# One block with 64 experts: half of the columns of each down projection as a split product of three fp32r matmuls, the other half left in fp32

## The chip, the cores and the metric

The kernel runs on one core of one Trainium2 chip. The metric is the device time of one execution in microseconds, the median of three runs. In the profile PE is the matrix engine (TensorE), PEld its weight loads, DVE VectorE, ACT ScalarE, POOL GpSimd, and SP the queue that issues the large loads from HBM.

## The reference

One layer over 512 tokens of 1024 values. First a mixing sub-layer (gated MLP beside stick-breaking attention), then the part that takes most of the time: a mixture of 64 experts, 8 of them for each token.

```python
h = rmsnorm(x, g_pre_ffn) * (1.0 + sc2) + sh2
gates = route(h, w_router, router_bias)            # 8 of 64 experts for each token
g = einsum('sd,edf->sef', h, w_gate)               # w_gate, w_up: (64, 1024, 256)
u = einsum('sd,edf->sef', h, w_up)
act = silu(g) * u * gates[:, :, None]
y = einsum('sef,efd->sd', act, w_down)             # w_down: (64, 256, 1024)
y = y + (silu(h @ ws_gate) * (h @ ws_up)) @ ws_down
x = x + ga2 * rmsnorm(y, g_post_ffn)
```

Everything is float32, and the three weights of an expert are 1 MB each.

## The kernel before

The five engines have their programs written out by hand, with semaphores between them. The experts are worked through as **blocks** of up to 128 rows: one block for each of the 64 experts, and further ones where an expert has more than 128 tokens. In this run there are 68 blocks. A block is `(i, s)` with number `b = 2i + s`, and `s` (0 or 1, `SLOTS = 2`) says which of two buffers it uses. `after(i, s, d)` is the block `d` further on, `num` its number.

What happens to block b:

1. SP (`refill`) loads the gate and up weights into `raw[:, s]` as soon as both halves of the low parts of block b-2 have been made (`split_done`: semaphores `lo_dve` and `lo_pool`). Right behind, in the same call, it loads the **down weights of block b-2** into `rawd[:, s]`, once the down projection of b-4 is over (`dn_mm`).
2. POOL gathers the rows of h for the block (`gather`, L580), by indices that DVE makes from a one-hot product (`tables`, `onehot`).
3. PE transposes the rows (`rows_in`, helper line L947). ACT takes their high part `hthi` (L859, a cast to fp32r), DVE the low part `htlo` (L1675).
4. ACT casts the raw gate and up weights to fp32r in two halves (`high`, L827: `whi`); DVE makes three quarters of each low half (`low`, L1661: `raw - whi`) and POOL the last quarter (`low_rest`, L595).
5. PE runs the **split product** (`gate_up`, L1213 to L1215): for each of 8 k tiles `hthi x whi`, `hthi x wlo`, `htlo x whi`, each a 128x512 fp32r matmul.
6. ACT applies silu (L855), DVE multiplies (L1668: `act_s`), PE transposes (`acts_tr`), ACT copies the result out of PSUM (`act_rows`, L863: `actt`).
7. PE runs the down projection (`down`, L1232): four fp32 matmuls of 128x512, two k tiles for each half of the 1024 columns, straight from `rawd`. The profile records each of them as two.
8. ACT copies the rows out (`y_out`, L869), POOL scatters them to `y_rows` (`scatter`, L588).

The engines are at different blocks in one step. The order of a step on each is fixed by these calls:

```python
# PE, block_pe(b)
rows_in(b+1); indices(b+3); gate_up(b, 0, 3); acts_tr(b-1); gate_up(b, 3, 8); down(b-1)
# ACT, step_act(b)
y_out(b-3); ht_high(b); high(b, 0); act_rows(b-2); high(b, 1); silu(b-1)
# DVE, step_dve(b)
rows_of(b-3); ht_low(b); tables(b+2); onehot(b+3); low(b, 0); low(b, 1); times_up(b-1)
# POOL, step_pool(b)
scatter(b-3); gather(b+2); low_rest(b, 0); low_rest(b, 1)
# SP, refill(b)
split_done(b-2); load gate, up (b); wait dn_mm >= b-3; load down (b-2)
```

So ACT, DVE and POOL work at step b while PE is in `block_pe(b-1)`. Each engine takes its list strictly in order.

Of the kernel before, what the change touches and what calls it, by code (L numbers as in the profile page):

```python
# [61 lines left out]
def block_kernel(nc, x, c, w_ada, b_ada, g_pre_mix, w_in, ln_sgu_g, ln_sgu_b, w_spatial, b_spatial,  # L62
                 g_branch, w_out, g_post_mix, g_pre_ffn, w_router, router_bias, w_gate, w_up,
                 w_down, ws_gate, ws_up, ws_down, g_post_ffn, out):
    with ExitStack() as ctx:
        def sem(name):
            return ctx.enter_context(nc.semaphore(name))
# [4 lines left out]
        def at(name, shape, dt, off):  # L72
            return nc.alloc_sbuf_tensor_at(name, shape, dt, offset=base + off)
# [3 lines left out]
        raw = at("raw", [P, SLOTS, 2, 2048], F32, 0)  # L77
        rawd = at("rawd", [P, SLOTS, KF, D], F32, 32 * KB)
        whi = at("whi", [P, SLOTS, 2, 2048], F32R, 48 * KB)
        wlo = [at("wlo0", [P, 2, 2048], F32R, 96 * KB), at("wlo1", [P, 2, 2048], F32R, 80 * KB)]  # L80
# [84 lines left out]
        act_s = small("act_s", [P, KF, P], F32)  # L165
        actt = at("actt", [P, KF, P], F32, 184 * KB)
        sht = at("sht", [P, 2, KF, P], F32, 64 * KB)

# [156 lines left out]
        at_tr = sem("at_tr")  # L325
        actt_ok = sem("actt_ok")
        dn_mm = sem("dn_mm")
        y_ok = sem("y_ok")
# [327 lines left out]
        def _(ac):  # L656
# [204 lines left out]
            def act_rows(i, s):  # L861
                ac.wait_ge(at_tr, num(i, s) + 1)
                A(actt[:, :, :], bank(3)[:, 0:F].rearrange("p (k q) -> p k q", k=KF), ACT.Copy).then_inc(actt_ok, 1)  # L863

            def y_out(i, s):
# [5 lines left out]
            def step_act(i, s, late):  # L871

                if late >= 3:
                    y_out(*after(i, s, -3))
                ht_high(i, s)
                high(i, s, 0)
                if late >= 2:
                    act_rows(*after(i, s, -2))
                high(i, s, 1)
                silu(*after(i, s, -1))  # L880
# [47 lines left out]
            last = m + (E // 2 - 1)  # L928
            y_out(m + (E // 2 - 2), 1)
            act_rows(last, 0)  # L930
            silu(last, 1)
            y_out(last, 0)
            act_rows(last, 1)
            y_out(last, 1)

# [7 lines left out]
        def _(pe):  # L943
# [281 lines left out]
            def down(i, s):  # L1225
                pe.wait_ge(wd_in[s], i * 16 + 16)
                pe.wait_ge(actt_ok, num(i, s) + 1)
                if not (isinstance(i, int) and num(i, s) == 0):
                    pe.wait_ge(y_ok, num(i, s))
                for hf in range(2):  # L1230
                    for k in range(KF):
                        ins = mm(bank(4 + hf), actt[:, k, :], rawd[:, s, k, hf * 512:(hf + 1) * 512],  # L1232
                                 start=(k == 0), stop=(k == KF - 1))
                ins.then_inc(dn_mm, 1)
# [68 lines left out]
        def _(v):  # L1303
# [354 lines left out]
            def low(i, s, half):  # L1658
# [3 lines left out]
                                ALU.subtract).then_inc(lo_dve, 1)  # L1662

            def times_up(i, s):

# [16 lines left out]

            def step_dve(i, s, late=True):
                if late:
                    rows_of(*after(i, s, -3))
                ht_low(i, s)
                tables(*after(i, s, 2))
                onehot(*after(i, s, 3))
                low(i, s, 0)
                low(i, s, 1)  # L1690
                times_up(*after(i, s, -1))
# [14 lines left out]
            over_tables()  # L1706
            step_dve(0, 1, late=False)
            step_dve(1, 0, late=False)
            for b in range(3, 6):
# [6 lines left out]
            with v.If(m > 0):  # L1716
                with v.Fori(E // 2, m + E // 2) as i:
                    for s in range(SLOTS):
                        step_dve(i, s)
            rows_of(m + (E // 2 - 2), 1)  # L1720
            times_up(m + (E // 2 - 1), 1)
            rows_of(m + (E // 2 - 1), 0)
            rows_of(m + (E // 2 - 1), 1)
# [43 lines left out]
```

## Time and profile before

| what | value |
|---|---|
| median of the runs | 1160.01 us (1159.15 to 1163.89) |
| the profiled execution | 1166.54 us, its span 1164.8 us |
| PE busy | 1007.2 us, 86% of the span |
| DVE / ACT / POOL busy | 744.7 / 569.7 / 615.8 us |
| DMA queue q1 (the loads of SP) | 267.41 MB |
| share of the chain that ended last | PE 75%, DVE 12%, DMA 4% |
| costliest line of that chain | L1232, the down projection, 19% |
| PE clock granted, mean of the span | 0.939 of 2.4 GHz |

The span runs from the first instruction to the last. A busy share tells only how much an engine had to do over the whole of it. The chain that ended last is followed back from the last instruction, and tells what the end waited for. From about 396 us to about 1076 us the kernel is in the loop over blocks.

### The profile page before, as it was taken

To read this page: it belongs to the slowest core of one execution; us is meant where nothing else is said; L and a number is where in the kernel's file an instruction comes from. 1 tells how busy PE (TensorE), PEld (TensorE's weight loads), DVE (VectorE), ACT (ScalarE), POOL (GpSimd) and SP (SyncE) were. 2 spreads that over 40 slices of the span, in tenths; PEclk is the share of its full clock that TensorE was granted. 3 is DMA by queue.
4 is the path that set the end of the run, shared out by engine and by line. 5 is a ranking of instruction groups with operands and counts; after the bars stand their busy time and mean duration, and the time that the engine had idled before them with its cause. 6 is when DMAs were issued, how large, how long until landed. Compare 5 with 4: busy or idle time off the path is not lost.

```text
span 1164.8 us, 14917 instructions
## 1 busy us (share of the span) xinstructions
PE 1007.2 (86%) x4420; PEld 711.0 (61%) x4420; DVE 744.7 (64%) x1287; ACT 569.7 (49%) x604; POOL 615.8 (53%) x364
## 2 busy tenths in 40 slices
PE   0699998979789999999999999999999999999100
PEld 0587775548554676666776666777666776666000
DVE  4649774743764856676676766666767665664387
ACT  4334135742341665565666565665655666564010
POOL 0233223540230676776767777767677777775250
PEclk9699998989899999999999999999999999999655
DMA  9647751211342689999999999999989888985681
GB/s 322 244 176 252 264 196 50 69 39 71 113 180 82 248 320 358 361 374 377 357 382 358 347 366 340 362 383 359 364 338 356 333 337 343 354 330 190 272 324 54
DMA packets 71399, 318.65 MB, mean 274 GB/s; under 512 B 18576, under 2 KB 19088, under 8 KB 44880
## 3 DMA queue, kind: packets, MB, share of 16 engines
q1 hardware_dynamic: 44592, 267.41, 60.3%
q0 software_dynamic: 23104, 47.50, 11.1%
q10 hardware_dynamic: 3680, 3.46, 0.9%
q8 instruction: 12, 0.20, 0.1%
q14 instruction: 11, 0.09, 0.0%
HBM read 317.25 MB, written 39.85 MB: 307 GB/s over the span
## 4 chain that ended last, share of the span: by engine, by line
PE 75%; DVE 12%; DMA 4%; issue 3%; ACT 3%; POOL 2%; SPq 0%; ACTq 0%; POOLq 0%; DVEq 0%
PE ps L1232 19%; PE ps L1213 10%; PE ps L1215 10%; PE ps L1214 10%; PE ps L947 8%; PE ps L998 7%; PE ps L1148 2%; DVE yall L1735 2%; PE ps L1123 2%; DVE acc L1346 1%; DMA rawd<-in_w_down_dram 1%; PE ps L1080 1%; PE ps L1054 1%; DMA ada<-in_w_ada_dram 1%; PE ps L1168 1%
## 5 line engine op out<-in xcount | busy, mean ns | idle before, releaser
L827 ACT ACTIVATE whi<-raw 128x2048 fp32r<-128x2048 f32 x136 | 260.4, 1915 | 33.1 <-DMA raw<-in_w_up_dram 16.7
L1661 DVE TENSOR_TENSOR wlo<-raw,whi 128x1536 fp32r<-128x1536 f32 x134 | 257.1, 1940 | 21.4 <-ACT whi L827 20.8
L580 POOL DMA_INDIRECT hg<-h_rows,idxg x70 | 186.6, 2666 | 141.9 <-DVE idxg L1655 141.6
L1232 PE MATMUL ps<-rawd,actt 128*128 128x512 f32 x544 | 245.0, 593 | 1.6 <-ACT actt L863 1.4
L595 POOL TENSOR_TENSOR wlo<-raw,whi 128x512 fp32r<-128x512 f32 x134 | 235.9, 1782 | 2.4 <-ACT whi L827 0.7
L1213 PE MATMUL ps<-whi,hthi 128*128 128x512 f32 x544 | 225.3, 414 | 1.8 <-POOL wlo L595 1.8
L1215 PE MATMUL ps<-whi,htlo 128*128 128x512 f32 x544 | 213.2, 392 | 0.0
L1214 PE MATMUL ps<-wlo,hthi 128*128 128x512 f32 x544 | 212.9, 391 | 0.0
L1675 DVE TENSOR_TENSOR htlo<-ps,hthi 128x1024 fp32r<-128x1024 f32 x68 | 83.3, 1225 | 196.7 <-ACT hthi L859 196.7
L869 ACT ACTIVATE ysb<-ps 128x1024 f32<-128x1024 f32 x68 | 69.6, 1024 | 205.7 <-PE ps L1232 205.7
L1232 PEld LDWEIGHTS ps<-rawd,actt 128*128 128x128 f32 x544 | 102.3, 189 | 106.2 <-issue 98.8
L588 POOL DMA_INDIRECT y_rows<-ysb,idxs x68 | 72.7, 1070 | 95.3 <-ACT ysb L869 64.5
L1215 PEld LDWEIGHTS ps<-whi,htlo 128*128 128x128 f32 x544 | 102.1, 188 | 23.3
L1213 PEld LDWEIGHTS ps<-whi,hthi 128*128 128x128 f32 x544 | 102.2, 188 | 19.3 <-issue 2.0
L1214 PEld LDWEIGHTS ps<-wlo,hthi 128*128 128x128 f32 x544 | 102.8, 189 | 17.2
L947 PEld LDWEIGHTS ps<-ident,hg 128*128 128x128 f32 x552 | 64.6, 141 | 34.9 <-issue 34.8
L947 PE MATMUL ps<-ident,hg 128*128 128x128 f32 x552 | 71.6, 273 | 0.0
L859 ACT ACTIVATE hthi<-ps 128x1024 fp32r<-128x1024 f32 x68 | 69.4, 1020 | 0.7 <-PE ps L947 0.7
L1346 DVE SCALAR_TENSOR_TENSOR acc<-ada,sc_col,acc 128x1024 f32<-128x1024 f32 x42 | 62.8, 1495 | 8.9 <-DMA ada<-in_w_ada_dram 7.6
L543 POOL TENSOR_TENSOR wplo<-wraw,wphi 128x1024 fp32r<-128x1024 f32 x10 | 30.1, 3012 | 66.0 <-ACT wphi L704 66.0
L1640 DVE TENSOR_SCALAR s_onehot<-iotab,posb 128x128 bf16<-128x128 bf16 x284 | 52.7, 250 | 0.0
L555 POOL TENSOR_TENSOR wolo<-woraw,wohi 128x512 fp32r<-128x512 f32 x16 | 36.1, 2274 | 31.3 <-ACT wohi L797 24.9
(245 smaller groups left out, 1312.7 us busy)
## 6 DMA issues: line engine op xcount, KB each, us to landing
raw<-in_w_gate_dram SPq DMA_DIRECT2D x68, 1024.0 KB, 7.7
raw<-in_w_up_dram SPq DMA_DIRECT2D x68, 1024.0 KB, 10.8
rawd<-in_w_down_dram SPq DMA_DIRECT2D x68, 1024.0 KB, 13.2
ada<-in_w_ada_dram SPq DMA_DIRECT2D x24, 1024.0 KB, 7.2
yall<-y_rows SPq DMA_DIRECT2D x8, 2048.0 KB, 22.4
wraw<-in_w_in_dram POOLq DMA_DIRECT2D x10, 1024.0 KB, 6.7
woraw<-in_w_out_dram SPq DMA_DIRECT2D x16, 256.0 KB, 2.8
xs<-in_x_dram SPq DMA_DIRECT2D x4, 512.0 KB, 10.9
```

The source lines that it names most:

```text
L580: gp.indirect_dma_start(out=hg[s][:, :, :].rearrange("p k q -> p (k q)"), out_offset=None, in_=h_rows, in_offset=bass.IndirectOffsetOnAxis ...
L595: gp.tensor_tensor(wlo[s][:, :, c0:c1], raw[:, s, :, c0:c1], whi[:, s, :, c0:c1].bitcast(F32), ALU.subtract).then_inc(lo_pool, 1)
L827: A(whi[:, s, :, cols], raw[:, s, :, cols], ACT.Copy).then_inc(hi_ok, 1)
L947: return pe.transpose(o, i, ident[:, :])
L998: ins = mm(bank(m), st, mv, start=(h == 0 and k == 0 and n == 0), stop=(h == 1 and k == KH - 1 and n == 2))
L1213: mm(out_, hthi[s][:, k, :], hi, start=(k == 0), stop=False)
L1214: mm(out_, hthi[s][:, k, :], lo, start=False, stop=False)
L1215: ins = mm(out_, htlo[s][:, k, :], hi, start=False, stop=(k == KD - 1))
L1232: ins = mm(bank(4 + hf), actt[:, k, :], rawd[:, s, k, hf * 512:(hf + 1) * 512], start=(k == 0), stop=(k == KF - 1))
L1346: ins = V.scalar_tensor_tensor(out=acc[:, ch % 2, :], in0=src, scalar=sc_col[:, k:k + 1], in1=acc[:, ch % 2, :], op0=ALU.mult, op1=ALU.add)
L1661: V.tensor_tensor(wlo[s][:, :, c0:c1], raw[:, s, :, c0:c1], whi[:, s, :, c0:c1].bitcast(F32), ALU.subtract).then_inc(lo_dve, 1)
L1675: V.tensor_tensor(htlo[s][:, :, :], bank(0, 2).rearrange("p (k q) -> p k q", k=KD), hthi[s][:, :, :].bitcast(F32), ALU.subtract).then_inc( ...
```

## The change

In `down`, the columns 512 to 1023 stay as they are (two fp32 matmuls, now first, into PSUM bank 5). The columns 0 to 511 become a split product into bank 4: with `dhi` and `dlo` the high and low part of the down weights, and `acthi`, `actlo` those of the activations, PE runs `acthi x dhi`, `acthi x dlo`, `actlo x dhi` for each of two k tiles, six fp32r matmuls.

The four operands are made so: ACT casts `dhi` from `rawd` (`down_high`, 128x1024) and `acthi` from PSUM (in `act_rows`, ahead of `actt`); DVE computes `dlo = rawd - dhi` over the raw weights in place (`down_low`, 128x1024) and `actlo = actt - acthi` (`act_low`, 128x256). `dhi`, `acthi`, `actlo` exist once, not once per slot.

```diff
+        dlo = at("dlo", [P, SLOTS, KF, D], F32R, 32 * KB)
+        dhi = at("dhi", [P, KF, 512], F32R, 116 * KB)
...
+        acthi = at("acthi", [P, KF, P], F32R, 189 * KB)
+        actlo = at("actlo", [P, KF, P], F32R, 190 * KB)
...
             def act_rows(i, s):
                 ac.wait_ge(at_tr, num(i, s) + 1)
+                if not (isinstance(i, int) and num(i, s) == 0):
+                    ac.wait_ge(dn_mm, num(i, s))
+                A(acthi[:, :, :], bank(3)[:, 0:F].rearrange("p (k q) -> p k q", k=KF), ACT.Copy).then_inc(acthi_ok, 1)
                 A(actt[:, :, :], bank(3)[:, 0:F].rearrange("p (k q) -> p k q", k=KF), ACT.Copy).then_inc(actt_ok, 1)
+
+            def down_high(i, s):
+
+                ac.wait_ge(wd_in[s], i * 16 + 16)
+                if not (isinstance(i, int) and num(i, s) == 0):
+                    ac.wait_ge(dn_mm, num(i, s))
+                A(dhi[:, :, :], rawd[:, s, :, 0:512], ACT.Copy).then_inc(dhi_ok, 1)
...
                 ht_high(i, s)
+                if late >= 2:
+                    down_high(*after(i, s, -2))
                 high(i, s, 0)
...
-                for hf in range(2):
-                    for k in range(KF):
-                        ins = mm(bank(4 + hf), actt[:, k, :], rawd[:, s, k, hf * 512:(hf + 1) * 512],
-                                 start=(k == 0), stop=(k == KF - 1))
+                for k in range(KF):
+                    mm(bank(5), actt[:, k, :], rawd[:, s, k, 512:D], start=(k == 0), stop=(k == KF - 1))
+                pe.wait_ge(dhi_ok, num(i, s) + 1)
+                pe.wait_ge(dlo_ok, num(i, s) + 1)
+                pe.wait_ge(actlo_ok, num(i, s) + 1)
+                for k in range(KF):
+                    for n, (a, w) in enumerate(((acthi[:, k, :], dhi[:, k, :]),
+                                                (acthi[:, k, :], dlo[:, s, k, 0:512]),
+                                                (actlo[:, k, :], dhi[:, k, :]))):
+                        ins = mm(bank(4), a, w, start=(k == 0 and n == 0), stop=(k == KF - 1 and n == 2))
                 ins.then_inc(dn_mm, 1)
...
+            def down_low(i, s):
+                v.wait_ge(dhi_ok, num(i, s) + 1)
+                V.tensor_tensor(dlo[:, s, :, 0:512], rawd[:, s, :, 0:512], dhi[:, :, :].bitcast(F32),
+                                ALU.subtract).then_inc(dlo_ok, 1)
+
+            def act_low(i, s):
+                v.wait_ge(actt_ok, num(i, s) + 1)
+                V.tensor_tensor(actlo[:, :, :], actt[:, :, :], acthi[:, :, :].bitcast(F32),
+                                ALU.subtract).then_inc(actlo_ok, 1)
...
                 onehot(*after(i, s, 3))
+                if late >= 2:
+                    down_low(*after(i, s, -2))
                 low(i, s, 0)
+                if late >= 2:
+                    act_low(*after(i, s, -2))
                 low(i, s, 1)
```

**ACT, one step of the loop.** Before:

```order
L869 ACTIVATE ysb_98<-ps 128x1024
L859 ACTIVATE hthi_93<-ps 128x1024
L827 ACTIVATE whi<-raw 128x2x1024
L863 ACTIVATE actt<-ps 128x256
L827 ACTIVATE whi<-raw 128x2x1024
L855 ACTIVATE sg<-ps 128x256
```

The same step with the change:

```order
L887 ACTIVATE ysb_100<-ps 128x1024
L867 ACTIVATE hthi_95<-ps 128x1024
L881 ACTIVATE dhi<-rawd 128x1024
L835 ACTIVATE whi<-raw 128x2x1024
L873 ACTIVATE acthi<-ps 128x256
L874 ACTIVATE actt<-ps 128x256
L835 ACTIVATE whi<-raw 128x2x1024
L863 ACTIVATE sg<-ps 128x256
```

The cast of the down weights of block b-2 stands ahead of both casts of the gate and up weights of block b. ACT had no instruction before that read `rawd`.

**DVE, the same step**, from the low part of the rows on. Before, with the four one-hot rows and the index rows between left out:

```order
L1675 TENSOR_TENSOR htlo_96<-ps,hthi_94 128x1024
L1655 TENSOR_SCALAR idxg_170<-destr 128x1
L1661 TENSOR_TENSOR wlo_52<-raw,whi 128x2x768
L1661 TENSOR_TENSOR wlo_52<-raw,whi 128x2x768
L1668 SCALAR_TENSOR_TENSOR act_s<-sg,slotv,ps 128x128x2
```

With the change:

```order
L1713 TENSOR_TENSOR htlo_98<-ps,hthi_96 128x1024
L1683 TENSOR_SCALAR idxg_174<-destr 128x1
L1694 TENSOR_TENSOR dlo<-rawd,dhi 128x2x512
L1689 TENSOR_TENSOR wlo_55<-raw,whi 128x2x768
L1699 TENSOR_TENSOR actlo<-actt,acthi 128x256
L1689 TENSOR_TENSOR wlo_55<-raw,whi 128x2x768
L1706 SCALAR_TENSOR_TENSOR act_s<-sg,slotv,ps 128x128x2
```

Two subtractions of two SBUF operands are added, one ahead of each half of the gate and up weights' low parts.

## Rows read from the trace of the kernel before

**Rows 1.** Busy time by stretch of the loop: PE, PEld, DVE, ACT, POOL, PEclk, DMA share, GB/s.

```profile
404.00:520.00 116.00, 116.00 (x520) 81.29 (x519) 78.72 (x144) 69.69 (x67) 83.48 (x46) 1.00 0.92 354
520.00:640.00 120.00, 119.96 (x542) 84.09 (x541) 79.24 (x155) 73.48 (x73) 84.42 (x47) 1.00 0.95 369
```

**Rows 2.** The chain that ended last, inside the loop: start us, us, what.

```profile
611.56 3.43 PE ps L1232 x8
614.99 0.87 PE ps L947 x8
...
620.66 0.23 PE ps L1214
620.88 0.23 PE ps L1215
...
621.79 3.43 PE ps L1232 x8
625.22 0.87 PE ps L947 x8
...
626.18 0.34 PE ps L1213
```

**Rows 3.** Timeline of PE: the down projections of the first and of the 64th block.

```profile
406.21 3.59 PE L1232 MATMUL ps<-rawd,actt 128*128 128x512 f32 x8
...
1052.55 3.59 PE L1232 MATMUL ps<-rawd,actt 128*128 128x512 f32 x8
```

**Rows 4.** The chain: a load of the down weights, and what waited for it.

```profile
648.25 14.53 DMA rawd<-in_w_down_dram
662.82 3.70 PE ps L1232 x8
```

**Rows 5.** Timeline of ACT, two PE blocks after the step at 637 us.

```profile
656.96 1.02 ACT L859 ACTIVATE hthi<-ps 128x1024 fp32r<-128x1024 f32 x1
659.89 1.92 ACT L827 ACTIVATE whi<-raw 128x2048 fp32r<-128x2048 f32 x1 [1.91 <-DMA raw<-in_w_up_dram]
661.71 0.36 ACT L863 ACTIVATE actt<-ps 128x256 f32<-128x256 f32 x1
```

**Rows 6.** Loads of down weights over the whole span (L436, x68).

```profile
DMA to landing us min/median/max: 4.8/13.2/15.3
```

**Rows 7.** Timeline: one step whose gate and up weights came late, to its refill.

```profile
588.03 1.92 ACT L827 ACTIVATE whi<-raw 128x2048 fp32r<-128x2048 f32 x1 [1.91 <-issue]
...
592.04 2.44 DVE L1661 TENSOR_TENSOR wlo<-raw,whi 128x1536 fp32r<-128x1536 f32 x1 [0.31 <-ACT whi L827]
...
590.03 5.59 POOL L595 TENSOR_TENSOR wlo<-raw,whi 128x512 fp32r<-128x512 f32 x2 [0.28 <-ACT whi L827]
...
595.84 0.33 SPq L432 DMA_DIRECT2D raw<-in_w_gate_dram  x1
596.26 0.38 SPq L433 DMA_DIRECT2D raw<-in_w_up_dram  x1
596.84 0.33 SPq L436 DMA_DIRECT2D rawd<-in_w_down_dram  x1
```

**Rows 8.** DMA issues of 900 to 950 us: count, KB, median us to landing.

```profile
DMA packets 3428, 16.51 MB, mean 330 GB/s; under 512 B 1240, under 2 KB 1240, under 8 KB 1586
...
raw<-in_w_up_dram SPq DMA_DIRECT2D x5, 1024.0 KB, 9.1
rawd<-in_w_down_dram SPq DMA_DIRECT2D x5, 1024.0 KB, 11.2
```

**Rows 9.** The same for the one block from 922 to 932 us.

```profile
raw<-in_w_gate_dram SPq DMA_DIRECT2D x1, 1024.0 KB, 4.8
raw<-in_w_up_dram SPq DMA_DIRECT2D x1, 1024.0 KB, 7.6
rawd<-in_w_down_dram SPq DMA_DIRECT2D x1, 1024.0 KB, 10.3
```

**Rows 10.** Timeline: DVE and POOL in an undisturbed step, and the refill before rows 4.

```profile
637.55 1.23 DVE L1675 TENSOR_TENSOR htlo<-ps,hthi 128x1024 fp32r<-128x1024 f32 x1 [3.67 <-ACT hthi L859]
...
640.09 3.42 DVE L1661 TENSOR_TENSOR wlo<-raw,whi 128x1536 fp32r<-128x1536 f32 x2
...
640.20 4.19 POOL L580 DMA_INDIRECT hg<-h_rows,idxg  x1 [1.73 <-DVE idxg L1655]
644.42 2.50 POOL L595 TENSOR_TENSOR wlo<-raw,whi 128x512 fp32r<-128x512 f32 x2
...
635.29 1.04 PE L947 MATMUL ps<-ident,hg 128*128 128x128 f32 x8
```

**Rows 11.** Timeline of POOL: the gather of the late step of rows 7.

```profile
588.75 1.01 POOL L580 DMA_INDIRECT hg<-h_rows,idxg  x1 [1.68 <-DVE idxg L1655]
```

More of the change, by code:

```diff
@@ L326, in block_kernel @@
         actt_ok = sem("actt_ok")
+        acthi_ok = sem("acthi_ok")
+        actlo_ok = sem("actlo_ok")
+        dhi_ok = sem("dhi_ok")
+        dlo_ok = sem("dlo_ok")
         dn_mm = sem("dn_mm")
@@ L929, in _ @@
             y_out(m + (E // 2 - 2), 1)
+            down_high(last, 0)
             act_rows(last, 0)
@@ L932, in _ @@
             y_out(last, 0)
+            down_high(last, 1)
             act_rows(last, 1)
@@ L1681, in rows_of, with step_dve @@
                 V.tensor_copy(idxs[s][:, :], col(destr, num(i, s))).then_inc(idxs_ok, 1)
-            def step_dve(i, s, late=True):
-                if late:
+            def step_dve(i, s, late=3):
+                if late >= 3:
                     rows_of(*after(i, s, -3))
@@ L1706, in _ @@
             over_tables()
-            step_dve(0, 1, late=False)
-            step_dve(1, 0, late=False)
+            step_dve(0, 1, late=1)
+            step_dve(1, 0, late=2)
             for b in range(3, 6):
@@ L1720, in _ @@
             rows_of(m + (E // 2 - 2), 1)
+            down_low(m + (E // 2 - 1), 0)
+            act_low(m + (E // 2 - 1), 0)
             times_up(m + (E // 2 - 1), 1)
+            down_low(m + (E // 2 - 1), 1)
+            act_low(m + (E // 2 - 1), 1)
             rows_of(m + (E // 2 - 1), 0)
```

## The prediction, made before the changed kernel ran

> **What bounds the kernel now.** I read the busy time by stretch first. Between 404 and 640 us PE is busy without a gap, at full clock, and the DMA engines are at a share of 0.92 to 0.95 [rows 1]. So two resources are nearly full at once, and a change that relieves PE must be checked against the loads. Then the chain that ended last: inside the loop it is PE alone, one down projection to the next in 621.79 - 611.56 = 10.23 us [rows 2]. Over 63 blocks, (1052.55 - 406.21) / 63 = 10.26 us each [rows 3], so stalls are rare. Third, the places where the chain leaves PE. One is a load of down weights: issued at 648.25, landed 14.53 us later, and PE's down projection started at 662.82, 0.04 us after it [rows 4]. That the loads come just in time is what the reader should keep from this view. Last, the timelines, for what each engine does in a step and who holds up whom.
>
> **PE's part.** The down projection is eight records in 3.43 us, 0.43 us each [rows 2]. Half of it, four records, is removed: 1.72 us. Six fp32r matmuls of 512 columns are added at 0.23 us each [rows 2], 1.37 us. PE's block gets shorter by 0.35 us, to 10.23 - 0.35 = 9.88. The first split matmul after another kind takes 0.34 instead of 0.23 us [rows 2], so the gain may be 0.24. With nothing else in the way, that is at most (10.26 - 9.88) x 66 blocks = 25 us.
>
> An fp32 matmul is thus 0.857 / 0.229 = 3.7 fp32r ones here. The Trainium skill (FP8 and Floating Point Precision, TensorE Precision Notes) counts four passes for true fp32; by four, the removed half would be 1.83 us and the gain 0.46 us a block. The row decides.
>
> **ACT's part.** Added are `dhi`, 128x1024, at the 1.02 us of `hthi`, a cast of the same size [rows 5], and `acthi` at the 0.36 us of `actt` [rows 5]. It has idle time for both. What matters is *where* the cast of `dhi` stands and what it waits for. It needs the down weights of block b-2 right behind `hthi` of step b, and both casts of the gate and up weights, `actt` and silu are queued behind it on ACT. The load of rows 4 was for a projection that PE starts at 662.82; ACT now wants it when `hthi` of that step ends, 656.96 + 1.02 = 657.98 [rows 5]. That is 4.8 us earlier, with a load that landed at 662.78. The median load takes 13.2 us from its issue [rows 6]: 648.25 + 13.2 = 661.45, still 3.5 us late. Before, ACT waited here only for gate and up weights, which land ahead of the down weights.
>
> **What the late cast does.** It closes a loop over two steps. The refill for block b is issued when the low parts of b-2 are done, and carries the down weights of b-2. With the change the casts for b wait for that landing; their low parts release the refill for b+2. So two steps take:
>
> - from the issue of the gate load to that of the down load: 596.84 - 595.84 = 1.0 us [rows 7];
> - the down load to its landing: L;
> - `dhi` with its semaphore: 1.02 + 0.05 = 1.07 us;
> - from the start of the first cast to the next refill. A step that began late shows it whole: 588.03 to 595.84, 7.81 us [rows 7];
> - `acthi` between the two casts: 0.36 us;
> - `actlo` on DVE ahead of the second low part: half of 3.42 = 1.71 us for 1536 elements [rows 10] makes 0.29 us for 256. DVE idles 0.31 us there [rows 7], so 0 to 0.3; I take 0.15.
>
> Sum: 1.0 + L + 9.4. For L the rows give 10.3 us when the queue is empty [rows 9] and 13.2 in the median [rows 6]. Half of the sum is the time of a step: 10.35 us with 10.3, 11.8 us with 13.2. I take L = 11.2, the median of the stretch from 900 to 950 us, where 330 GB/s were moved [rows 8]. The reason is that the loop's own pace fixes the traffic: the bytes of rows 1 (354 to 369 GB/s, mean 362, times 10.23 us = 3.7 MB a block) in 10.8 us make 343 GB/s, nearest to that stretch. So a step takes (1.0 + 11.2 + 9.4) / 2 = **10.8 us**.
>
> DVE's two additions and PE's wait for them lie inside this. `actt` is ready 1.07 + 1.92 + 0.36 + 0.36 = 3.7 us after the landing; PE then runs its fp32 half for 1.72 us, while DVE's `dlo` is long done (1.3 us from `dhi`, priced at 1.71 x 1024 / 1536 = 1.14 to 1.23 [rows 10]).
>
> **The sum.** (10.80 - 10.26) x 66 blocks = +36 us. The prologue and the tail are untouched but for the last block, where `acthi` and the shorter projection cancel. Against the profiled execution (1166.5 us) that is 1202; against the median of 1160.0 it is **1196 us**. A change of over 0.5% (5.8 us) is about what the measurement can tell from none.
>
> **Rivals.**
>
> *The port, not the load* (slower, smaller). The gather on POOL takes 4.19 us when it runs beside DVE's low parts and ends 0.9 us after them [rows 10], but 1.01 us when DVE is idle [rows 11]. `dlo` and `actlo` lengthen that stretch by 1.14 + 0.29 = 1.43 us, so the gather and POOL's first low part end later. Now that part ends 644.42 + 1.25 - 635.29 = 10.4 us after the block's start [rows 10], and PE may need it at one period plus 626.18 - 625.22 = 0.96 us [rows 2]. With 11.8 needed and 9.88 + 0.96 = 10.84 there, 1.0 us is missing. The stall itself delays the next start, so half of it remains: 10.4 us a step, +0.14 x 66 = +9 us, 1169 us. For it: the rows show the hold-up plainly. Against it as the decider: where the casts come late, the gather slips in before the low parts, as in rows 11. It decides if L stays below 10.4.
>
> *The loads keep up* (faster). It decides if L falls below 9.4, since (1.0 + 9.4 + 9.4) / 2 = 9.9, PE's own block. PE then gains all its 0.35 us and the time is 1160 - 25 = 1135. For it: an empty queue landed the gate load in 4.8 us [rows 9], and the rate may have room. Against: even that empty queue needed 10.3 us for the down load [rows 9], and a faster PE asks for more bytes in less time.
> The Trainium skill (HBM Reference, its table of specifications and the text under it) gives a core that streams alone about 425 GB/s; by it the 3.15 MB of a block's weights would take an estimated 7.4 us, and the loads would keep up. The busiest stretch here shows 369 GB/s at a DMA share of 0.95.
>
> *Nothing moves* (within 0.5%). L of about 10.1 puts the loop at 10.25 us, today's pace: 1160.
>
> *The queue stays full* (much slower). If L stays at its median of 13.2 although the pace drops, the step is 11.8 us and the time 1160 + 1.54 x 66 = 1262. Against: a slower pace drains the queue.
>
> That the change is not doing what it says can be left out: each engine's order is fixed by hand and the listing shows the new operations.
>
> **Chances.** The two-step loop with L between 10.4 and 12.5: 0.63. The port: 0.13. The queue stays full: 0.06. Nothing moves: 0.08. Faster: 0.10. So slower by over 0.5% has 0.82, within 0.5% 0.08, faster 0.10. The predicted time is the likeliest case's. Its own bounds are L = 10.3 (10.35 us, 1166) and L = 12.5 (11.45 us, 1239). The range is widened down to 1160 to take in the port and half of the unmoved case, and ends at 1240: it leaves out the faster case, the full queue and a rest, about 0.2.
>
> **What would show it.** Right: ACT idles for some 2 to 3 us ahead of `dhi` in nearly every step, released by the DMA of `rawd`; the steps are near 10.8 us; PE waits ahead of its down projection for `actt`; the down load's median falls to about 11 us and the mean rate to about 340 GB/s; the gather takes 1.0 us in most steps. PE's fp32 half should be four records of 0.43 us and its split half six of 0.23. Wrong: ACT not waiting for `rawd`, a DMA share above 0.95 with steps of 9.9 us (then the loads kept up), or PE waiting before its first gate matmul for POOL's `wlo` with gathers of 5 us (then it is the port).

## The result, and the profile after

The changed kernel takes 1225.88 us (median of 4 runs, 1223.43 to 1230.99), the kernel before 1161.95 in the same comparison (4 runs, 1159.15 to 1165.08): a ratio of 1.0545, with a 95% interval of 1.0501 to 1.0588. The forecast was 1196 us, in a range of 1160 to 1240. So the sign and the range held, but the loss is 64 us where 36 were forecast.

The page of the changed kernel: span and busy time, the chain by engine and by line, and the three weight loads (the last number of a load is its median from issue to landing, in us).

```profile
span 1221.7 us, 15727 instructions
...
PE 1002.6 (82%) x4556; PEld 735.0 (60%) x4556; DVE 900.2 (74%) x1423; ACT 650.6 (53%) x740; POOL 627.5 (51%) x364
...
PE 27%; DMA 20%; issue 18%; DVE 18%; ACT 8%; POOL 5%; SPq 2%; ACTq 1%; POOLq 0%; DVEq 0%
...
raw<-in_w_gate_dram SPq DMA_DIRECT2D x68, 1024.0 KB, 5.4
raw<-in_w_up_dram SPq DMA_DIRECT2D x68, 1024.0 KB, 8.4
rawd<-in_w_down_dram SPq DMA_DIRECT2D x68, 1024.0 KB, 11.1
```

PE was the chain nearly alone before (75% of the span in the page's chain; DMA 4%). Now PE has 27%, and loads, DVE and the gaps between instructions share the rest. The down load lands 11.1 us after its issue, where the median was 13.2 [rows 6]: the queue is less full.

Busy time by stretch, with the columns of [rows 1]:

```profile
404.00:520.00 116.00, 103.43 (x487) 75.73 (x485) 98.20 (x152) 73.71 (x79) 69.46 (x41) 1.00 0.86 323
520.00:640.00 120.00, 111.58 (x528) 82.50 (x527) 99.31 (x165) 79.80 (x88) 82.05 (x44) 1.00 0.90 347
```

Against [rows 1], PE is idle for 12.6 and 8.4 us where it had no gap, the clock is at its upper level of 2.4 GHz in both, and the loads run below their former rate. Nothing here is full. That is the picture of a loop of waits, not of an engine that became too slow.

Now the pace: the timeline's rows of the second and of the 66th down projection, then the chain's two rows of one block.

```profile
405.31 1.88 PE L1253 MATMUL ps<-rawd,actt 128*128 128x512 f32 x4
...
1117.83 1.88 PE L1253 MATMUL ps<-rawd,actt 128*128 128x512 f32 x4
```

```profile
707.66 1.72 PE ps L1253 x4
709.38 1.40 PE ps L1261 x6
```

The 64 steps between these two down projections took (1117.83 - 405.31) / 64 = 11.13 us each; before, it was 10.26. The two chain rows are PE's own block: 1.72 + 1.40 = 3.12 us where 3.43 stood [rows 2], as priced. So 0.87 us a step was lost although PE's work shrank. 64 x 0.87 = 56 us, which is all of the spans' difference (1221.7 - 1164.8 = 57); the medians differ by some 7 us more than the two profiled executions do.

The steps are not alike. Of the 64, 37 take 10.5 to 11.1 us, eight 9.9 to 10.2, nine 11.2 to 12.0 and ten 12.2 to 13.3. Who waits, in the loop (us in total, times, longest):

```profile
ACT dhi L881 <- DMA rawd<-in_w_down_dram: 77.3, 53, 3.8
...
PE ps L1261 <- DVE actlo L1699: 21.3, 33, 0.8
PE ps L1253 <- issue: 16.7, 12, 2.6
...
PE ps L1235 <- POOL wlo L603: 12.0, 15, 1.0
PE ps L1253 <- ACT actt L874: 10.7, 13, 1.5
```

The first row is the predicted wait: ACT stands ahead of `dhi` for the down weights 53 times. But PE's own waits have three causes: `actt` is late with the cast, `actlo` is DVE, and `wlo` is POOL. The row that ends in "issue" belongs to `actt` too: in each of its 12 cases PE starts 0.10 us after `actt` is written. So `actt` stands for 27.4 us over 25 steps. One late step on the timeline shows the first two:

```profile
737.93 1.06 ACT L881 ACTIVATE dhi<-rawd 128x1024 fp32r<-128x1024 f32 x1 [2.27 <-DMA rawd<-in_w_down_dram]
738.90 1.90 ACT L835 ACTIVATE whi<-raw 128x2048 fp32r<-128x2048 f32 x1
...
741.57 1.98 PE L1253 MATMUL ps<-rawd,actt 128*128 128x512 f32 x4 [1.13 <-ACT actt L874]
...
740.83 1.76 DVE L1689 TENSOR_TENSOR wlo<-raw,whi 128x1536 fp32r<-128x1536 f32 x1 [0.58 <-ACT whi L835]
742.51 1.50 DVE L1699 TENSOR_TENSOR actlo<-actt,acthi 128x256 fp32r<-128x256 f32 x1
...
740.88 4.26 POOL L603 TENSOR_TENSOR wlo<-raw,whi 128x512 fp32r<-128x512 f32 x2 [1.59 <-ACT whi L835]
...
744.15 0.47 PE L1261 MATMUL ps<-dhi,acthi 128*128 128x512 f32 x1 [0.60 <-DVE actlo L1699]
...
746.94 0.33 SPq L440 DMA_DIRECT2D raw<-in_w_gate_dram  x1
```

ACT idles for 2.27 us, casts `dhi`, and only then the weights, whose low parts release the refill at 746.94. PE's fp32 half starts after 1.13 us of waiting for `actt`. Then comes something that the forecast lacks: `actlo` takes 1.50 us, and the split half of the down projection waits 0.60 us for it. It subtracts 256 elements a partition; alone it takes 0.42 us. POOL's low part began at 740.88, 0.05 us behind DVE's. POOL's row holds two subtractions of 1.25 us each [rows 10] in 4.26 us. By these durations the first waits until DVE's ends near 742.6, and then DVE's `actlo` waits for POOL's. Of the 68 `actlo`, 35 take 1.49 us and 33 take 0.42.

Where `actlo` is short, something else is long. This is a step in which the down weights are only a little late:

```profile
703.24 1.06 ACT L881 ACTIVATE dhi<-rawd 128x1024 fp32r<-128x1024 f32 x1 [0.56 <-DMA rawd<-in_w_down_dram]
704.21 1.90 ACT L835 ACTIVATE whi<-raw 128x2048 fp32r<-128x2048 f32 x1
...
705.37 3.99 POOL L588 DMA_INDIRECT hg<-h_rows,idxg  x1 [1.36 <-DVE idxg L1683]
...
708.05 0.42 DVE L1699 TENSOR_TENSOR actlo<-actt,acthi 128x256 fp32r<-128x256 f32 x1
...
709.38 3.26 POOL L603 TENSOR_TENSOR wlo<-raw,whi 128x512 fp32r<-128x512 f32 x2
...
712.87 0.33 SPq L440 DMA_DIRECT2D raw<-in_w_gate_dram  x1
```

The gather is issued beside DVE's row of subtractions, takes 3.99 us instead of 1.01, and POOL's low parts, which release the refill, end last. From the first weight cast to the refill it is 712.87 - 704.21 = 8.66 us; in the late step above it was 746.94 - 738.90 = 8.04. Over the 60 casts of `dhi` that start between 404 and 1080 us:

| steps | ACT idle ahead of `dhi` | gather | `actlo` | first weight cast to refill, mean |
|---|---|---|---|---|
| 32 | 0.8 to 3.8 | 1.0 to 2.1 | 1.49 | 8.03 |
| 28 | 0 to 0.75 | 4.0 to 5.7 (one of 1.5) | 0.42 | 9.49 |

So the long way to the refill belongs to the held gather, and not to the long `actlo`.

### The profile page after: what moved, and what is told of

Read it like the earlier page. It is cut to its first block, busy times and chain, and to the rows that moved or that the text cites. A ratio compares the mean times of both kernels' runs of the same rounds, so it can differ in the third digit from the quotient of the medians.

```text
span 1221.7 us, 15727 instructions
## 1 busy us (share of the span) xinstructions
PE 1002.6 (82%) x4556; PEld 735.0 (60%) x4556; DVE 900.2 (74%) x1423; ACT 650.6 (53%) x740; POOL 627.5 (51%) x364
## 3 DMA queue, kind: packets, MB, share of 16 engines
q0 software_dynamic: 23104, 47.50, 10.6%
## 4 chain that ended last, share of the span: by engine, by line
PE 27%; DMA 20%; issue 18%; DVE 18%; ACT 8%; POOL 5%; SPq 2%; ACTq 1%; POOLq 0%; DVEq 0%
DMA rawd<-in_w_down_dram 18%; PE ps L1020 7%; POOL wlo L603 3%; PE ps L1261 3%; ACT whi L835 3%; DVE wlo L1689 3%; PE ps L1170 2%; PE ps L969 2%; DVE actlo L1699 2%; DVE yall L1781 2%; PE ps L1145 2%; ACT hthi L867 2%; PE ps L1253 1%; PE ps L1235 1%; DVE acc L1374 1%
## 5 line engine op out<-in xcount | busy, mean ns | idle before, releaser
L1689 DVE TENSOR_TENSOR wlo<-raw,whi 128x1536 fp32r<-128x1536 f32 x134 | 275.8, 2059 | 16.3 <-ACT whi L835 15.8
L588 POOL DMA_INDIRECT hg<-h_rows,idxg x70 | 202.1, 2886 | 107.9 <-DVE idxg L1683 100.4
L603 POOL TENSOR_TENSOR wlo<-raw,whi 128x512 fp32r<-128x512 f32 x134 | 232.0, 1752 | 42.1 <-ACT whi L835 41.0
L1235 PE MATMUL ps<-whi,hthi 128*128 128x512 f32 x544 | 224.4, 412 | 13.6 <-POOL wlo L603 13.3
L1253 PE MATMUL ps<-rawd,actt 128*128 128x512 f32 x272 | 132.3, 610 | 30.1 <-issue 16.7
L881 ACT ACTIVATE dhi<-rawd 128x1024 fp32r<-128x1024 f32 x68 | 72.1, 1060 | 77.6 <-DMA rawd<-in_w_down_dram 77.3
L1694 DVE TENSOR_TENSOR dlo<-rawd,dhi 128x1024 fp32r<-128x1024 f32 x68 | 83.1, 1223 | 25.3 <-ACT dhi L881 25.1
L1253 PEld LDWEIGHTS ps<-rawd,actt 128*128 128x128 f32 x272 | 49.3, 190 | 77.2 <-issue 74.1
L1261 PE MATMUL ps<-dhi,acthi 128*128 128x512 f32 x136 | 70.5, 519 | 21.3 <-DVE actlo L1699 21.3
L1374 DVE SCALAR_TENSOR_TENSOR acc<-ada,sc_col,acc 128x1024 f32<-128x1024 f32 x42 | 62.4, 1486 | 11.9 <-DMA ada<-in_w_ada_dram 10.6
## 6 DMA issues: line engine op xcount, KB each, us to landing
rawd<-in_w_down_dram SPq DMA_DIRECT2D x68, 1024.0 KB, 11.1
xs<-in_x_dram SPq DMA_DIRECT2D x4, 512.0 KB, 10.6
```

The lines of the kernel that those rows point to most:

```text
L588: gp.indirect_dma_start(out=hg[s][:, :, :].rearrange("p k q -> p (k q)"), out_offset=None, in_=h_rows, in_offset=bass.IndirectOffsetOnAxis ...
L603: gp.tensor_tensor(wlo[s][:, :, c0:c1], raw[:, s, :, c0:c1], whi[:, s, :, c0:c1].bitcast(F32), ALU.subtract).then_inc(lo_pool, 1)
L1235: mm(out_, hthi[s][:, k, :], hi, start=(k == 0), stop=False)
L1253: mm(bank(5), actt[:, k, :], rawd[:, s, k, 512:D], start=(k == 0), stop=(k == KF - 1))
L1261: ins = mm(bank(4), a, w, start=(k == 0 and n == 0), stop=(k == KF - 1 and n == 2))
L1689: V.tensor_tensor(wlo[s][:, :, c0:c1], raw[:, s, :, c0:c1], whi[:, s, :, c0:c1].bitcast(F32), ALU.subtract).then_inc(lo_dve, 1)
```

## The experiments

The theory was the two-step loop: ACT wants the down weights too early. The rival was the port: DVE's subtractions from SBUF and POOL's work (its gather, its own subtractions) hold each other up. The first four kernels take one or the other away, or add one alone to the kernel before. Leaving out the subtractions takes away DVE's own work as well as the hold-up; experiment 11, which keeps all of the work, shows that the work by itself is not what costs. All ratios are against the kernel before on the same chip.

**1. The cast later.** `dhi` is cast behind `actt`, between the two casts of the gate and up weights, and `dlo` follows `actlo`. All work stays.

```diff
 step_act:
-                if late >= 2:
-                    down_high(*after(i, s, -2))
                 high(i, s, 0)
                 if late >= 2:
                     act_rows(*after(i, s, -2))
+                    down_high(*after(i, s, -2))
 step_dve:
-                if late >= 2:
-                    down_low(*after(i, s, -2))
                 low(i, s, 0)
                 if late >= 2:
                     act_low(*after(i, s, -2))
+                    down_low(*after(i, s, -2))
```

> The changed kernel with the cast of the down weights moved on ACT to behind actt, between the two casts of the gate and up weights, and its low part on DVE moved behind actlo. Nothing is left out, the operations are the same. Load loop (the early need of the down weights sets the step): the load may now land 2.6 us later, and only the second cast, not both, is behind it; (1.0 + 11.5 + 1.0 + about 6.5) / 2 = 10.0 us, so PE and the port decide: a step of 9.9 to 10.5 us, 1137 to 1176 us, ACT idle for rawd near 0. Port (the two subtractions on DVE hold POOL up): the subtractions are still there, so the step stays near 11.1 us and the time within 1205 to 1230 us.

Measured: 1193.55 us (4 runs, 1188.1 to 1201.7), ratio 1.0259 [1.0207, 1.0312]. About half of the loss is gone; the time lies in neither of the two ranges that were expected. Its waits, and its timeline with the gather in one step:

```profile
PE ps L1234 <- POOL wlo L603: 29.4, 30, 2.3
...
ACT dhi L881 <- DMA rawd<-in_w_down_dram: 6.0, 11, 1.2
```

```profile
700.53 5.74 POOL L588 DMA_INDIRECT hg<-h_rows,idxg  x1 [1.68 <-DVE idxg L1682]
706.30 2.52 POOL L603 TENSOR_TENSOR wlo<-raw,whi 128x512 fp32r<-128x512 f32 x2
...
700.50 1.75 DVE L1688 TENSOR_TENSOR wlo<-raw,whi 128x1536 fp32r<-128x1536 f32 x1
702.16 0.42 DVE L1698 TENSOR_TENSOR actlo<-actt,acthi 128x256 fp32r<-128x256 f32 x1
702.50 1.22 DVE L1693 TENSOR_TENSOR dlo<-rawd,dhi 128x1024 fp32r<-128x1024 f32 x1
703.63 1.75 DVE L1688 TENSOR_TENSOR wlo<-raw,whi 128x1536 fp32r<-128x1536 f32 x1
...
707.72 0.47 PE L1234 MATMUL ps<-whi,hthi 128*128 128x512 f32 x1 [0.93 <-POOL wlo L603]
```

The wait for the down weights fell from 77.3 to 6.0 us, and what is left is the rival, as it was described: DVE runs four subtractions without a gap from 700.50 to 705.38, the gather takes 5.74 us and ends 0.9 us after them, POOL's first low part comes late, and PE waits 0.93 us ahead of its gate matmul. Of the 64 steps 26 take 9.9 to 10.2 us, 25 take 10.6 to 11.1, mostly in turns, and 12 are longer (mean 10.66). So the two causes are both there, and each hides a part of the other.

**2. The wait alone.** In the kernel before, ACT waits for the down weights behind `hthi` and does nothing with them; products and casts are those of before.

```diff
+            def down_high(i, s):
+                ac.wait_ge(wd_in[s], i * 16 + 16)
...
                 ht_high(i, s)
+                if late >= 2:
+                    down_high(*after(i, s, -2))
                 high(i, s, 0)
```

> The kernel before, with one wait added on ACT behind the cast of hthi: for the down weights of the block two back, where the change waits for them. No operation is added. Load loop: issue to issue 1.0 us, load 11.5, then 7.8 to 8.8 us to the next refill, half of the sum is 10.2 to 10.7 us a step: 1160 to 1190 us, with ACT idle for rawd in most steps. Port: no subtraction is added, so 1160 us.

**3. The wait and the cast.** The same with the cast of `dhi`, which nobody uses but which PE's down projection waits for.

```diff
                 ac.wait_ge(wd_in[s], i * 16 + 16)
+                if not (isinstance(i, int) and num(i, s) == 0):
+                    ac.wait_ge(dn_mm, num(i, s))
+                A(dhi[:, :, :], rawd[:, s, :, 0:512], ACT.Copy).then_inc(dhi_ok, 1)
```

> As the run with the wait alone, and the cast of dhi (128x1024) behind the wait; nobody uses the cast, PE runs the four fp32 matmuls as before. Load loop: 1.0 us more in two steps than with the wait alone, half of it a step: +0.5 us a step, +33 us over that run, 1190 to 1220 us. Port: no subtraction is added, so 1160 us.

**4. The changed kernel without DVE's two subtractions.** `dlo` and `actlo` are left out; PE does its six matmuls on `acthi` and `dhi`.

```diff
-                                                (acthi[:, k, :], dlo[:, s, k, 0:512]),
-                                                (actlo[:, k, :], dhi[:, k, :]))):
+                                                (acthi[:, k, :], dhi[:, k, :]),
+                                                (acthi[:, k, :], dhi[:, k, :]))):
...
-                if late >= 2:
-                    down_low(*after(i, s, -2))
                 low(i, s, 0)
-                if late >= 2:
-                    act_low(*after(i, s, -2))
```

> The changed kernel without the two subtractions on DVE: PE multiplies acthi and dhi three times over, in place of the products with the low parts, so the matmuls are the same six; the low parts are left out. Load loop: the stretch from the first cast to the refill is shorter by the 0.4 us that actlo costs, (1.1 + 11.4 + 1.0 + 8.2) / 2 = 10.85 us a step, about 1200 us; ACT still idles for rawd. Port: without them PE's own block of 9.9 us is left, 1137 us.

Measured: the wait alone 1192.28 us (1179.12 to 1194.74), ratio 1.0211 [1.0144, 1.0277]; wait and cast 1209.0 (1201.7 to 1215.6), 1.0360 [1.0317, 1.0404]; without DVE's part 1205.73 (1198.93 to 1211.6), 1.0360 [1.0308, 1.0411]. With the wait alone, ACT waits for the down weights like this (the first cast stands behind it; 104.5 us over 49 steps in the second kernel, 102.6 over 55 in the third):

```profile
ACT whi L829 <- DMA rawd<-in_w_down_dram: 113.3, 54, 4.5
```

A wait that computes nothing costs 2.1% on its own (just above the range that was expected). With the cast behind it the loss is 3.6%, with nothing new on DVE and no new work on PE. The changed kernel without DVE's part has the same 3.6% although PE's block is 0.35 us shorter there. Its median is 3 us lower, less than the runs of either scatter, so no gain from the shorter block can be told while the loop binds. And DVE's part makes 1.036 into 1.0545, 1.8 points more. Experiments 3 and 4 are the two-step loop in a pure form: 11.04 and 10.85 us a step, with gathers of 1.01 us in all but one step.

**5. Both taken away.** The cast at its later place and no subtractions on DVE (low parts left out as in the one above).

> The moved casts of the run before (dhi between the two casts of the gate and up weights) and no subtraction on DVE; PE multiplies acthi and dhi three times over, the low parts are left out. If the load's place and DVE's subtractions are the two causes and there is no third, both are gone and PE's own block is left: 9.9 us a step but for late loads, 1137 to 1150 us. If the load alone is the cause, it is no faster than the run with the moved casts (1190 us).

Measured: 1151.03 us (1144.6 to 1155.98), ratio 0.9858 [0.9807, 0.9909], 1 us above the range that was expected; most steps 9.9 to 10.0 us, mean 10.09. Of the four cases it is the only one in which most steps are PE's own block of 9.88. Both casts are still made here, so ACT's added work by itself is not the cause. With it the two causes stand in a square: both 1.0545, the port only 1.026, the load only 1.036, neither 0.986. Against 0.986 the port alone costs 4.0 points, the load alone 5.0, and both together 6.9: they overlap, so that taking away one gives back less than it costs alone.

**6. The load earlier.** The casts stay where the change puts them. SP issues the down load ahead of the gate and up loads, behind the wait for the down projection of b-4 alone, so it no longer waits for the low parts.

```diff
 refill:
-                split_done(num(*after(i, s, -2)))
-                load_gate_up(e, s)
                 sp.wait_ge(dn_mm, num(*after(i, s, -3)))
                 load_down(e_down, s)
+                split_done(num(*after(i, s, -2)))
+                load_gate_up(e, s)
```

> The changed kernel with one change in the order of SP's queue: the load of the down weights is issued as soon as its buffer is free, ahead of the wait for the low parts and of the gate and up loads. Load loop: the down weights land 2.7 us or more earlier, the need of dhi no longer closes the loop, the up load does: (0.4 + 10.8 + 8.8) / 2 = 10.0, and the port's 10.4 decides: 1170 to 1190 us, ACT idle for rawd under 0.4 us a step. Port alone: the order on SP changes nothing, 1226 us.

Measured: 1194.55 us (1193.32 to 1197.26), ratio 1.0254 [1.0227, 1.0281]. DMA issues of the loop (404 to 1050 us), and the wait that is left:

```profile
rawd<-in_w_down_dram SPq DMA_DIRECT2D x61, 1024.0 KB, 6.9
raw<-in_w_gate_dram SPq DMA_DIRECT2D x61, 1024.0 KB, 8.5
```

```profile
PE ps L1235 <- POOL wlo L603: 24.7, 27, 1.2
```

The down load lands in 6.9 us, ACT's wait for it is no longer among the long ones, and the result is that of the first experiment by another road: 1.025 and the port. It is a little above the 1170 to 1190 us that were expected. Two independent edits that both end the wait for the down weights give the same gain.

**7. Both of these at once.** The later cast with the earlier load.

> Moved casts and the early load of the down weights together, both subtractions on DVE in place. The load has no part left; the port theory says 10.4 us a step, 9.9 and 10.9 in turns, 1170 us. If a remainder of late loads was in the run with the moved casts (1193 us, mean step 10.66), it goes: 1165 to 1180 us.

Measured: 1198.71 us (1194.26 to 1205.11), ratio 1.0298 [1.0248, 1.0347]. No better than either alone, and above the expected 1165 to 1180: the load cause can be removed only once, and the port costs more than the 10.4 us a step on which this expectation stood (10.76 measured).

**8. Room for the gather, first try: the one-hot rows later.** On top of 7, DVE makes its four one-hot rows behind the first low part, and takes `actlo` from PSUM.

```diff
-                onehot(*after(i, s, 3))
                 low(i, s, 0)
+                onehot(*after(i, s, 3))
...
-                V.tensor_tensor(actlo[:, :, :], actt[:, :, :], acthi[:, :, :].bitcast(F32),
+                V.tensor_tensor(actlo[:, :, :], bank(3)[:, 0:F].rearrange("p (k q) -> p k q", k=KF),
+                                acthi[:, :, :].bitcast(F32),
```

> As the run with moved casts and early load, and two things for the port: on DVE the one-hot rows stand behind the first low part instead of ahead of it, which leaves POOL's gather a window of 0.9 us between two subtractions of SBUF operands; and actlo is read from PSUM, not from actt. Port theory: the gather ends some 3 us earlier, POOL's first low part is ready before PE needs it, 9.9 to 10.1 us a step, 1137 to 1150 us: faster than both kernels. Otherwise it stays at 1170 us.

Measured: 1378.71 us (1375.59 to 1384.44), ratio 1.1838 [1.1795, 1.1882]: far off what was expected. Its timeline in one step, and its stretch of the loop with the columns of [rows 1]:

```profile
712.25 1.79 POOL L588 DMA_INDIRECT hg<-h_rows,idxg  x1 [1.93 <-DVE idxg L1682]
...
713.15 3.63 DVE L1667 TENSOR_SCALAR s_onehot<-iotab,posb 128x128 bf16<-128x128 bf16 x4
...
714.07 2.49 POOL L603 TENSOR_TENSOR wlo<-raw,whi 128x512 fp32r<-128x512 f32 x2
...
718.35 0.47 PE L1260 MATMUL ps<-dhi,acthi 128*128 128x512 f32 x1 [2.24 <-DVE dlo L1693]
```

```profile
404.00:1050.00 646.00, 543.23 (x2313) 404.97 (x2312) 516.24 (x723) 359.28 (x389) 257.43 (x193) 0.91 0.72 277
```

The gather did get its room (1.79 us). But the one-hot rows, four operations that take 0.74 us elsewhere, now lie beside POOL's two subtractions and take 3.63 us; they end 0.2 us after POOL's. `actlo` and `dlo` are queued behind them, and PE waits 2.24 us for `dlo`. That wait adds up to 142.3 us in 66 steps, two thirds of the 214 us that the kernel lost.

**9. Room for the gather, second try: POOL's order.** The gather goes behind POOL's first low part; once on the kernel of 1, once on that of 6.

```diff
 the POOL step:
-                gather(*after(i, s, 2))
                 low_rest(i, s, 0)
+                gather(*after(i, s, 2))
```

> The moved casts (load need relieved) with one change on POOL: the gather for two blocks ahead stands behind POOL's first low part instead of ahead of it. Nothing is left out. Port theory: PE waits for that first low part, which had to wait for the gather, which had to wait for the end of DVE's subtractions; now the first low part needs only the latter, 0.9 us earlier, and PE's wait of 1.0 us every other step goes: 9.9 to 10.1 us a step, 1140 to 1160 us. If DVE's own time is the bound and not the gather in the port's queue, it stays at 1190 us.

> The changed kernel with the early load of the down weights and the same change on POOL, the casts where the change has them. Port theory: as before the second run of the same pair, 1140 to 1165 us; PE may wait a little for actlo, which is made behind the first low part. Otherwise 1194 us as with the early load alone.

Measured: on the kernel of 1, 1258.81 us (1258.12 to 1262.72), ratio 1.0809 [1.0781, 1.0837], steady steps of 11.6 to 11.7 us; on that of 6, 1184.24 us (1182.15 to 1191.48), 1.0172 [1.0128, 1.0215]. The same edit loses 5.5 points on one and gains 0.8 on the other; neither expectation had a place for the first, and the second lies between its two. The timeline of the first shows why:

```profile
717.07 1.28 POOL L603 TENSOR_TENSOR wlo<-raw,whi 128x512 fp32r<-128x512 f32 x1 [0.95 <-ACT whi L835]
717.09 1.81 DVE L1667 TENSOR_SCALAR s_onehot<-iotab,posb 128x128 bf16<-128x128 bf16 x4
...
720.37 1.32 POOL L603 TENSOR_TENSOR wlo<-raw,whi 128x512 fp32r<-128x512 f32 x1 [0.83 <-ACT whi L835]
720.49 1.48 DVE L1698 TENSOR_TENSOR actlo<-actt,acthi 128x256 fp32r<-128x256 f32 x1
```

POOL's subtraction starts 0.02 us ahead of the one-hot rows and 0.12 us ahead of `actlo`, and both wait for it. Where `dlo` is made behind `actlo` (the kernel of 1), PE's wait for it grows to 1.6 us; where it is made earlier (6), only `actlo` is late, and PE waits at most 0.8 us.

**10. DVE's small tables first.** On the kernel of 6, the tables, which hold `idxg` for the gather, go ahead of `htlo`. `htlo` reads PSUM and SBUF, so a gather that starts then should find POOL's way free.

```diff
-                ht_low(i, s)
                 tables(*after(i, s, 2))
+                ht_low(i, s)
```

> The changed kernel with the early load of the down weights, and on DVE the gather's indices made ahead of htlo instead of behind it. Nothing is left out. The gather may then start about 2 us earlier, while DVE reads PSUM for htlo, and end before the subtractions of SBUF operands. If the held gather is what makes POOL's low part late, the steps of 10.9 go, a gather takes 1.0 us, and the time falls from 1194 to 1145 to 1170 us. If POOL's low parts, once free, get in between DVE's and hold up dlo and actlo, as where the gather stood behind, it stays within 1170 to 1195 us with PE waiting for actlo.

Measured: 1183.49 us (1182.23 to 1188.16), ratio 1.0174 [1.0151, 1.0197]. The gather's median is now 1.01 us, and PE's wait for `wlo` is gone from the long ones. This is the second of the two outcomes that were expected: the gain is small, and PE's longest wait in total is this one:

```profile
PE ps L1261 <- DVE actlo L1699: 18.7, 30, 1.0
```

`actlo` still has a median of 1.49 us. From 410 to 1050 us PE is idle for 22.7 us.

**11. What PE waits for, before POOL wakes.** On top of 10, ACT makes `acthi` and `actt` ahead of both weight casts, and DVE makes `actlo` right behind `dlo`, ahead of its own first low part. POOL's subtractions can't start before the first weight cast, so `actlo` meets none of them.

```diff
 step_act:
-                high(i, s, 0)
                 if late >= 2:
                     act_rows(*after(i, s, -2))
+                high(i, s, 0)
 step_dve:
-                low(i, s, 0)
                 if late >= 2:
                     act_low(*after(i, s, -2))
+                low(i, s, 0)
```

> As the run with the indices first, and acthi and actt cast ahead of the first cast of the gate and up weights, actlo made right behind dlo, ahead of the first low part. All that PE's down projection needs is made before POOL has anything to subtract, so POOL cannot get in between, and PE needs the first low parts only a block later. Both causes gone with all work done: 9.9 to 10.1 us a step, 1137 to 1155 us, faster than the kernel before. If a third cause is left, it is slower than 1160 us.

Measured: **1146.09 us** (6 runs, 1140.71 to 1149.07) against 1164.4 (11 runs), ratio **0.9828** [0.9805, 0.9851]. It computes all that the changed kernel computes. Its loop in one stretch, and one step on the timeline:

```profile
404.00:1050.00 646.00, 644.09 (x3120) 491.24 (x3120) 569.45 (x973) 486.90 (x519) 497.54 (x262) 1.00 0.96 362
```

```profile
705.24 1.01 POOL L588 DMA_INDIRECT hg<-h_rows,idxg  x1 [0.30 <-issue]
708.69 5.63 POOL L603 TENSOR_TENSOR wlo<-raw,whi 128x512 fp32r<-128x512 f32 x2 [2.44 <-ACT whi L835]
...
705.42 1.22 DVE L1694 TENSOR_TENSOR dlo<-rawd,dhi 128x1024 fp32r<-128x1024 f32 x1
706.55 0.42 DVE L1699 TENSOR_TENSOR actlo<-actt,acthi 128x256 fp32r<-128x256 f32 x1
708.64 4.52 DVE L1689 TENSOR_TENSOR wlo<-raw,whi 128x1536 fp32r<-128x1536 f32 x2 [1.66 <-ACT whi L835]
```

PE is idle for 1.9 of 646 us, the steps take 9.94 us in the mean, and the DMA share is 0.96. The subtractions of DVE and POOL are still in each other's way (4.52 us for DVE's two instead of 3.42, 5.63 for POOL's), but nobody that PE waits for stands behind them. From 10 to 11 the gain is 3.5 points. PE's idle time of 410 to 1050 us falls from 22.7 to 1.9 us, 3.2% of that stretch, and most of it was the wait for `actlo`. Which of the two orders, ACT's or DVE's, brings how much of it was not taken apart.

Not tried: the earlier load in the kernel before, and the order of the loads alone (the down load first, with both waits in place).

## Why the prediction was right, and where it fell short

The direction, the range and the waiting load came as forecast. The loss is 64 us where 36 were forecast. Of what the sum for a step lacks, one half is the load, which takes longer in the mean than the median that was put in; the other half is the held gather, which the working set to nothing.

**PE's part: right.** 3.12 us a block was forecast and measured, and the best version runs at 9.94 us a step where 9.88 was PE's own sum. That gain exists, but the changed kernel can't collect it.

**The loop over two steps: right as the mechanism.** The wait stands ahead of `dhi` in 53 of 64 steps; adding the wait alone to the old kernel costs 2.1%, wait and cast 3.6%; moving the cast or the load takes 2.9 points off. The forecast of ACT idle "2 to 3 us in nearly every step" was too high: 77.3 / 53 = 1.5 us. The traffic fell to 329 GB/s over 404 to 1050 us where 340 were forecast.

**The terms of the sum.** Measured on the timeline, in the mean over the 62 casts of `dhi` between 404 and 1120 us:

| term | forecast | measured |
|---|---|---|
| gate issue to down issue | 1.0 | 1.06 |
| down issue to `dhi` (L) | 11.2 | 11.58 (median 11.28) |
| `dhi` to the first weight cast | 1.07 | 0.96 |
| first cast to the refill | 7.81 + 0.36 + 0.15 = 8.32 | 8.73 |
| half of the sum | 10.8 | 11.16 |

L was taken near its median, but the mean is 0.4 us higher, and this is half of what is missing. The other half is the last term, and in it the gather. Where the gather is over early, the stretch is 8.03 us, less than forecast although `actlo` takes 1.49 us; where the gather is held, it is 9.49. Without DVE's two subtractions it is 7.83 us in the mean with `acthi` (experiment 4), and 7.80 without it (experiment 3). So `acthi` adds nothing where 0.36 us was put down, `actlo` some 0.2 us for 0.15, and the held gather 1.5 to 1.7 us in 28 of 60 steps for nothing. Experiment 4 has the forecast 10.8 us a step (10.85), but by luck: its L is 11.9 us and its last term 7.83, and the two errors cancel.

**"DVE's two additions and PE's wait for them lie inside this": wrong for the wait, nearly right for the loop.** PE waited for `actlo` 33 times (21.3 us), because it is not ready when the fp32 half is done. The price of 0.29 us came from the element count; alone it takes 0.42, and beside POOL's subtraction 1.49. The question who else wants the port at that moment was asked of the gather alone. The two-step loop hardly feels it (0.2 us), but once the load is in time it is what PE waits for (experiments 9 and 10).

**The port as a rival: wrongly set.** It was held against the load, at 1169 us and "where the casts come late, the gather slips in". That is so in 32 of 60 steps; in the 28 others the load was at most 0.75 us late, and in all but one of them the gather was held. So both are at work in the same kernel in turn: where the load is in time the port decides, and the reverse. Both signs that were to tell them apart appeared together. As an only cause it costs 2.6%, not the 0.8% that was worked out: 25 of its steps last some 10.9 us, the 1.0 us more that was worked out, but 12 are longer still, and the mean is 10.66 and not 10.4. The gather takes 1.0 us in 26 of 64 steps of the changed kernel, not in most of them.

The Trainium skill (SBUF — State Buffer, section "SBUF: two separate sides") says that VectorE and GpSimd share a port pair as an exclusive lock: whichever starts first holds it for the whole instruction, and the other is fully blocked. Of VectorE's operations this holds in a two-port mode, or with two SBUF inputs against a GpSimd operation that reads SBUF. The traces agree with it in both directions for the subtractions: `actlo` takes 0.42 us or, behind POOL's, 1.49, and POOL's first low part 1.28 us or, behind DVE's, 2.84. The one-hot rows (0.74 or 3.63) agree if they run in such a mode, which no run here shows. The page adds that a `tensor_tensor` was not seen to stall a DMA; here the gather, a DMA issued by POOL, took 1.01 us alone and up to 5.74 beside four of them, and the measurement decides.

**"The loads keep up": excluded for this kernel, true for the best one.** It was tied to a faster landing (L below 9.4). The way out was another: nothing lands faster, but the need is moved. In experiment 11 the rate is 362 GB/s, the same as in [rows 1].

## What to carry to other kernels

An operation that is added to an engine's order moves the need for its input to that place: before pricing its duration, compare that time with the landing of its load, and see what queues behind it. A wait there, with no work at all, cost 2.1%. Of an order on engines that share a resource, put first what the bottleneck waits for, at a time when the competitor can't have started yet; the amount of shared work can stay as it is. And where two causes each fit the trace, take both away before judging either: one alone gave back half here, and the gain of the change appeared only without both. Last, look at an operation's durations one by one and not at their median: `actlo` and the gather each had two or more, and only beside the length of each step did they tell which one cost time.

## What the runs showed that was not expected

- A small operation on DVE can cost many times its size by its place. `actlo` went from 0.42 to 1.49 us and the four one-hot rows, which have one SBUF source in bf16 and a column of scalars, from 0.74 to 3.63 us beside POOL's subtractions.
- A gather issued beside a row of DVE subtractions was held, in steps of 5.7 us, until the last of them ended, and 0.9 us beyond (experiment 1), though there are three borders between them at which it might have got in. In other steps it did get in: the one of 3.99 us shown above ends 0.9 us behind the third subtraction, another of 2.07 us behind the first. What decides between them stays open.
- In experiment 8 PE's clock fell. Between 690 and 700 us the granted clock was 1.00 (2.4 GHz); PE then waited 2.29 us for `dlo`, and from 705 to 710 us the mean was 0.72, with split matmuls starting 0.43 us apart instead of 0.23, which is the lower level of 1.2 GHz. The changed kernel's single waits of PE reach 2.6 us, and its mean clock stayed at 1.00 from 404 to 1050 us; there they are rare, here there is one in each step. In the first kernel of experiment 9 there is one in nearly each step too (53, up to 1.6 us), and the mean clock stayed at 1.00. So a part of the 18% is the clock, and not the wait itself.
